# Moving operand buffers placed 128 instead of 64 bytes past the weight slots, modulo 256

## What is computed

```python
def swiglu(h, w_gu, w_down):
    g, u = jnp.split(h @ w_gu, 2, axis=-1)
    return (jax.nn.silu(g) * u) @ w_down
```

## Time and profile before

| | |
|---|---|
| median of three runs | 4584.36 us |
| the profiled execution, its own time | 4610.93 us |
| its span, first to last instruction | 4609.1 us |
| mean granted TensorE clock | 0.944 of full speed |
| TensorE busy | 4164.6 us, 90% |
| GpSimd busy | 2665.2 us, 58% |
| matmuls on lines 638 and 617 | 26,256 |

### The profile page before, as it was taken

How to read it: one execution, slowest core, us unless ns; L and a number is a source line. 1 busy time by engine, 2 the same in 40 slices (tenths; PEclk the granted TensorE clock), 3 DMA queues, 4 the chain that set the end, 5 groups by cost and what they waited for, 6 DMA issues and landing times.

```text
span 4609.1 us, 94606 instructions
## 1 busy us (share of the span) xinstructions
PE 4164.6 (90%) x36305; PEld 3797.8 (82%) x36305; DVE 1600.6 (35%) x3002; ACT 1935.0 (42%) x2635; POOL 2665.2 (58%) x1186
## 2 busy tenths in 40 slices
PE   6899798899789889889999988899789999998799
PEld 5555798899589745589899987899689899987799
DVE  4422312412731442331212175214832212138521
ACT  3211345543344321144545455444545454435453
POOL 4000586486258500068678765687378787864576
PEclk9899899999799889999999998999899999998899
DMA  5245465365146534446556544565256565643454
GB/s 152 83 134 152 119 184 150 92 185 146 49 119 187 139 90 134 134 133 196 151 169 188 169 122 123 153 181 151 70 158 184 154 185 166 187 142 101 127 164 146
DMA packets 1177129, 664.73 MB, mean 144 GB/s; under 512 B 30141, under 2 KB 1138441, under 8 KB 1176743
## 3 DMA queue, kind: packets, MB, share of 16 engines
q1 hardware_dynamic: 1176871, 661.06, 49.7%
HBM read 659.92 MB, written 1.05 MB: 143 GB/s over the span
## 4 chain that ended last, share of the span: by engine, by line
PE 71%; issue 13%; POOL 7%; DVE 5%; ACT 2%; SPq 1%; DMA 1%; POOLq 0%; DVEq 0%; ACTq 0%
PE bank L638 54%; POOL wlo L541 7%; PE bank L967 5%; PE bank L718 2%; PE bank L617 1%; PE bank L801 1%; PE bank L1065 1%; PE bank L1059 1%; PE bank L1036 1%; DVE RSTD L724 1%; DVE W L740 1%; PE bank L874 1%; PE bank L1067 1%; PE bank L1042 0%; DVE AL L696 0%
## 5 line engine op out<-in xcount | busy, mean ns | idle before, releaser
L541 POOL TENSOR_TENSOR wlo<-raw,whi 128x1024 fp32r<-128x1024 f32 (+3 forms) x1182 | 2665.0, 2273 | 1919.7 <-ACT whi L551 1916.3
L638 PE MATMUL bank<-AH,whi 128*128 128x256 f32 x6320 | 1817.8, 288 | 193.4 <-DVE AL L696 103.9
L638 PE MATMUL bank<-AL,whi 128*128 128x256 f32 x6320 | 1798.9, 285 | 0.0
L638 PE MATMUL bank<-AH,wlo 128*128 128x256 f32 x6320 | 1798.2, 285 | 0.0
L551 ACT ACTIVATE whi<-raw 128x1024 fp32r<-128x1024 f32 (+3 forms) x1182 | 1172.1, 994 | 1211.5 <-PE bank L638 1053.8
L638 PEld LDWEIGHTS bank<-AH,whi 128*128 128x128 f32 x6320 | 1220.7, 193 | 212.0 <-issue 181.9
L638 PEld LDWEIGHTS bank<-AL,whi 128*128 128x128 f32 x6320 | 1224.2, 194 | 0.1
L638 PEld LDWEIGHTS bank<-AH,wlo 128*128 128x128 f32 x6320 | 1222.2, 193 | 0.0
L638 PE MATMUL bank<-HH,wlo 128*128 128x256 f32 x1936 | 541.0, 279 | 0.0
L638 PE MATMUL bank<-HH,whi 128*128 128x256 f32 x1936 | 540.8, 279 | 0.0
L638 PE MATMUL bank<-HL,whi 128*128 128x256 f32 x1936 | 540.5, 279 | 0.0
(11 more groups left out here) (334 smaller groups left out, 4326.1 us busy)
## 6 DMA issues: line engine op xcount, KB each, us to landing
raw<-in_ffn_w SPq DMA_DIRECT2D x420, 512.0 KB, 3.8
raw<-in_w_in SPq DMA_DIRECT2D x182, 512.0 KB, 3.9
raw<-in_ffn_w_gu SPq DMA_DIRECT2D x176, 512.0 KB, 3.8
raw<-in_w_ada SPq DMA_DIRECT2D x144, 512.0 KB, 4.4
raw<-in_ffn_w_down SPq DMA_DIRECT2D x64, 512.0 KB, 4.1
raw<-in_rw_w_rkv SPq DMA_DIRECT2D x48, 512.0 KB, 4.2
raw<-in_ffn_w SPq DMA_DIRECT2D x56, 384.0 KB, 3.4
raw<-in_ds_w_in SPq DMA_DIRECT2D x28, 512.0 KB, 3.7
```

What stands on the lines that cost most here:

```text
L541: pool.tensor_tensor(wlo[slot][:, 0:n], raw[slot][:, 0:n], whi[slot][:, 0:n], ALU.subtract).then_inc(lo_ready, 1)
L638: mm = pe.matmul(ps[:, 0:o.shape[2]], w, o[:, k0 + c, :], start=tile not in started and c == n == 0, stop=last_panel and c == nk - 1 and n ...
```

## The change

One number: the gap ahead of `AH` grows from 64 to 128 bytes.

```diff
         X = sb("X", C * S)
         CTX = sb("CTX", C * S)
-        place[0] += 64
+        place[0] += 128
         a_at = place[0]
         AH, AL = sb("AH", C * S, F32R), sb("AL", C * S, F32R)
         place[0] += 64
         cst = sb("cst", sum(n for _, n in CONST_AT.values()))
```

## The result

The changed kernel takes 4617.4 us, the median of twelve runs (4604.39 to 4635.69), against 4587.58 us for the kernel before, also of twelve. The ratio is 1.0062 with a 95% interval of 1.0045 to 1.0079: slower, by 21 to 36 us. The forecast was 4530 us and faster. The profiled execution of the kernel before is a long one: its 4610.93 us lie above all twelve of its timed runs (4579.58 to 4602.29), so the two profiles are closer to each other than the medians.

What follows compares the result with a forecast made beforehand. TensorE's dense matmul pace was taken as the bound: 54 us saved on dense matmuls, nothing for fp32, nothing taken back, so 4584.4 - 54 = 4530 us. The range was 4470 to 4690 us, faster at 0.42.

Steps and rivals of the forecast that it cites:

- The bound: Whole kernel: TensorE, busy 90% of the span, sets the time, with 54% of the last-ending chain over L638's dense matmuls.
- The term: Dense matmuls of L638 and L617: some 24,000 at the slow pace, half of them turning quick, 54 us saved.
- the two stable rhythms: Dense matmuls: two paces 4.5 ns apart, and a stretch keeps the one it starts with.
- the price at 128: Dense matmuls at the new distance: not in the trace, taken as half at the quick pace, 54 us saved.
- the nearest rows: Eight windows of L617 at distance -64, four quick and four slow, taken as the model for the new distance.
- the third: Feed-forward windows: a third pace that no row shows yet would prove the forecast wrong.
- period of 128: Rival on L638: SBUF repeats every 128 bytes, so 128 acts as 0; 4.5 ns more per matmul, 4692 us; chance 0.30.
- The end at all quick: Dense matmuls: disturbance shrinks with distance, so all 24,000 go to 113.3 ns, 108 us saved, 4476 us; chance 0.15.
- The rival of no effect: Dense matmuls: by the rule of independent SBUF ports the offset changes nothing, 4584 us; chance 0.28.
- The fp32 terms: Plain fp32 matmuls (L1470, L718, L874): moved or changed distance by 64, costed at nothing, 2 us either way.
- That nothing takes the gain back: Dense panels: GpSimd keeps 286 ns spare per panel, nothing is late, so what TensorE saves the kernel saves.

Runs made afterwards that it cites:

- gap 0: Gap ahead of AH set to 0 bytes instead of the 64 of the kernel before; 4634.3 us, ratio 1.0116.
- gap 192: Gap ahead of AH set to 192 bytes instead of the 64 of the kernel before; 4531.61 us, ratio 0.9872.
- gap 96: Gap ahead of AH set to 96 bytes instead of the 64 of the kernel before; 4636.34 us, ratio 1.0114.

## Why the prediction was wrong

**The bound was right.** The dense matmuls' pace sets the time: what they lost, 30 us, is what the median lost. The term's count, some 24,000 to 25,000 matmuls, held. The pace read from windows, 117.8 and 113.3 ns, held too, and so did the two stable rhythms.

**The step that failed is the price at 128.** I had no row at that distance and took those of L617, "the nearest rows", half quick and half slow, for 54 us saved. They were of the distance -64, and for -64 they were right: 4530 us was predicted for 128, and 4531.61 us was measured at 192. That the two agree within 2 us is partly luck, since one feed-forward more or less at the quick pace is 7 us by the prediction's own price. At 128 a matmul costs 1.2 ns more instead of 2.2 ns less, and no stretch is quick: of the prediction's signs of being wrong it was the third, a pace that no row had shown. The error was to read "another distance than +64" as if all others were alike; in a function with period 256 a row at -64 says nothing of 128. With that row alone both signs stood open. That 4617 us lies between the prediction's 4470 and 4690 is no merit of the forecast either: the high side was the price of the period of 128, a mechanism that fell.

**Where "farther is better" came in.** The end at all quick, 0.15, assumed that two streams disturb each other less the farther apart they start. The table is against it: 32 and 64 beat 128, and 96 is as bad as 0.

**The rival of no effect.** It fell: gap 0, after and gap 192 differ by more than their intervals with the same instructions. The Trainium skill's rule of two independent SBUF ports ("TensorE: Matmul & The Clock Gate", "Step-by-step: what each phase is for") isn't borne out as a statement on pace: at full clock the distance between the moving block and the weight block moves it from 115.5 to 120.0 ns. The rule may still hold for bandwidth in the large: no matmul came near the 217 ns of one after the other.

**The rival with a period of 128.** Its sign was right and its mechanism wrong: distances 0 and 128 have different paces and patterns (120.0 flat, 118.7 in a cycle of five), and 64 and 192 differ by 1.3% in time. Its price, 4.5 ns a matmul, was nearly four times too large.

**The fp32 terms.** Put at nothing, and they stayed. The norm's matmuls after the change:

```profile
L718 PE MATMUL bank<-W,ones x16: 377/379/379, 872.6 to 875.8; 128*128 128x256 f32 x16
```

16 in 3.2 us, 3.3 in the earlier trace rows; the distance stayed 64 there, as `ones` moved along. L1470, both of whose buffers moved, also keeps its 3.2 us. The line that tests the zero is L874, where `CTX` stayed and `la` moved, so that the distance went from -64 to 128:

```profile
L874 PE MATMUL bank<-CTX,la x16: 379/379/430, 110.5 to 113.8; 128*64 128x256 f32 x16
```

It keeps its 3.3 us of the earlier trace rows.

**That nothing takes the gain back** was not tested by the change, since it was slower; at gap 192 the gain of the pace did come through in full (1.15% by the pace, 1.28% measured), so GpSimd's spare of 286 ns per panel was enough.

**What stays open.** That it is the weight load which the moving stream meets is shown by elimination: the distance to whi and wlo counts, that to raw doesn't, nor does the absolute address. GpSimd and ScalarE also write whi and wlo, and I did not run a kernel without these writes. The traces speak against them: over the dense starts at full clock at which neither engine has an instruction running, some 900 in each profile, the mean distance is 119.8 ns at gap 0, 119.9 at gap 96, 118.7 after and 117.2 before, against 120.0, 119.9, 118.8 and 117.6 over all dense starts. So I take the weight load to be it. Why the cycle has five steps at 128 and six at 96, and what chooses between 113.3 and 117.8 at the start of a stretch, I can't say.

## What to carry to other kernels

Where TensorE is saturated, look at the distances between starts, not only at busy time. Here a pace above columns over clock that repeated in a fixed pattern came with an offset between buffers, and the offset was worth sweeping over one whole period, since neither neighbours nor opposite points foretold each other. A row taken as "nearest" must be nearest in the quantity that changes. Here the sweep gave a kernel 1.3% faster (gap 192, 0.9832 to 0.9912) from the same single number.

## What the runs showed of the hardware

- With 256 columns of fp32r against a load of 128 columns at 2.4 GHz, a matmul takes from 113.3 to about 120 ns, against 106.7 by columns alone, by the distance of the two start addresses modulo 256 bytes. 16 bytes are enough to move it: 115.5 ns at 192, 118.4 at 208, 119.2 at 176.
- At one and the same distance there can be two or three lasting rhythms, each held for a whole feed-forward of some 1500 matmuls: 113.3 or 117.8 ns at 192 (five and six of eleven feed-forwards), 118.7 or 120.0 at 128 (ten and one), 118.7, 117.3 or 120.0 at 160 (seven, three and one). At 0, 96, 176 and 224 all eleven had one pace. An estimate from the first pair: a feed-forward that falls the other way is worth some 7 us (1556 x 4.5 ns), with nothing else changed.
- Where only AH's distance changed, the pace changed in mid-stream with the buffer, 118.8 to 117.6 ns.
- Plain fp32 matmuls of 256 columns kept their pace of 16 starts in 3.3 us when their distance went from -64 to 128 (L874).
